# Expert weights by accumulating indirect DMAs into a DRAM table, in place of one-hot products per token

## The reference

```python
def chunk(xc):                                   # 128 tokens; PEER_HEADS = 8, PEER_KEYS = 128, PEER_TOPK = 16
    qh = (xc @ w_query).reshape(PEER_CHUNK, PEER_HEADS, PEER_QDIM)
    s1, s2 = ...                                 # scores against the two halves of the sub-keys
    v1, i1 = lax.top_k(s1, PEER_TOPK)
    v2, i2 = lax.top_k(s2, PEER_TOPK)
    cand = (v1[..., :, None] + v2[..., None, :]).reshape(PEER_CHUNK, PEER_HEADS, 256)
    vs, ci = lax.top_k(cand, PEER_TOPK)
    e1 = jnp.take_along_axis(i1, ci // PEER_TOPK, axis=-1)
    e2 = jnp.take_along_axis(i2, ci % PEER_TOPK, axis=-1)
    idx = e1 * PEER_KEYS + e2                    # one of 16384 experts
    g = jax.nn.softmax(vs, axis=-1)
    z = jnp.einsum('td,thkd->thk', xc, u_experts[idx])
    a = gelu(z) * g
    return jnp.einsum('thk,thkd->td', a, v_experts[idx])
```

## Time and profile before

| | before |
|---|---|
| median of 3 runs, us | 1976.41 (1974.06 to 1978.56) |
| span of the profiled execution, us | 1975.5 |
| mean granted clock of TensorE, share of full | 0.974 |
| PE busy, us | 1858.1 (94%) |
| DVE busy, us | 1457.3 (74%) |
| ACT busy, us | 860.9 (44%) |
| Pool busy, us | 30.0 (2%) |

### The profile page before, as it was taken

One profiled execution on the slowest core, in us unless ns is written; L12 is line 12 of the kernel. 1 busy time (PEld: TensorE's weight loads), 2 busy tenths in 40 slices (PEclk: granted clock), 3 DMA queues, 4 the chain that ended last, 5 costly groups with the idle time before them and its releaser, 6 DMA issues.

```text
span 1975.5 us, 36620 instructions
## 1 busy us (share of the span) xinstructions
PE 1858.1 (94%) x12406; PEld 1700.7 (86%) x12406; DVE 1457.3 (74%) x2826; ACT 860.9 (44%) x1255; POOL 30.0 (2%) x56
## 2 busy tenths in 40 slices
PE   5999899979998999779887999999999999999997
PEld 5999799969997999668776999999999888888885
DVE  4876556658756666665776699998888899996665
ACT  4344344434443444434544455543333333334443
POOL 0000000000000011000000000000000000000000
PEclk9999899989998999979998999999999999999999
DMA  5655465544444777553465455554444444445554
GB/s 189 206 169 181 144 211 185 186 132 163 158 154 146 254 245 214 172 169 123 155 211 193 138 172 180 174 179 137 138 138 138 135 142 148 139 149 172 194 194 142
DMA packets 91534, 334.14 MB, mean 169 GB/s; under 512 B 10697, under 2 KB 10857, under 8 KB 91010
## 3 DMA queue, kind: packets, MB, share of 16 engines
q1 hardware_dynamic: 86976, 314.23, 48.5%
q0 software_dynamic: 3504, 14.69, 2.3%
q10 hardware_dynamic: 978, 4.20, 0.6%
HBM read 330.95 MB, written 6.05 MB: 171 GB/s over the span
## 4 chain that ended last, share of the span: by engine, by line
PE 42%; DVE 12%; issue 2%; ACT 2%; DMA 0%; DVEq 0%; ACTq 0%; SPq 0%
PE bank L183 12%; PE bank L185 12%; PE bank L184 12%; DVE Z L82 5%; PE bank L1274 5%; DVE w_lo L164 4%; ACT w_hi L162 1%; DVE xn L82 1%; PE bank L402 1%; DVE st L82 0%; PE bank L347 0%; DVE rows_a L1259 0%; PE bank L237 0%; DMA raw<-stream 0%; PE bank L1114 0%
## 5 line engine op out<-in xcount | busy, mean ns | idle before, releaser
L164 DVE TENSOR_TENSOR w_lo<-raw,w_hi 128x1024 fp32r<-128x1024 f32 x594 | 718.8, 1222 | 227.3 <-ACT w_hi L162 218.4
L162 ACT ACTIVATE w_hi<-raw 128x1024 fp32r<-128x1024 f32 x594 | 624.7, 1053 | 286.2 <-PE bank L185 253.8
L183 PE MATMUL bank<-u_hi,w_hi 128*128 128x256 f32 x2416 | 700.7, 290 | 10.9 <-DVE cw L82 3.2
L184 PE MATMUL bank<-u_lo,w_hi 128*128 128x256 f32 x2416 | 687.5, 285 | 0.0
L185 PE MATMUL bank<-u_hi,w_lo 128*128 128x256 f32 x2416 | 687.1, 284 | 0.0
L183 PEld LDWEIGHTS bank<-u_hi,w_hi 128*128 128x128 f32 x2416 | 467.1, 193 | 22.8 <-issue 14.3
L184 PEld LDWEIGHTS bank<-u_lo,w_hi 128*128 128x128 f32 x2416 | 467.3, 193 | 4.8 <-issue 2.4
L185 PEld LDWEIGHTS bank<-u_hi,w_lo 128*128 128x128 f32 x2416 | 467.0, 193 | 0.0
L183 PE MATMUL bank<-w_hi,a_hi 128*128 128x512 f32 x768 | 306.6, 399 | 1.9 <-DVE a_lo L1321 1.9
L184 PE MATMUL bank<-w_lo,a_hi 128*128 128x512 f32 x768 | 300.2, 391 | 0.0
L185 PE MATMUL bank<-w_hi,a_lo 128*128 128x512 f32 x768 | 299.8, 390 | 0.0
(11 more groups left out here) (207 smaller groups left out, 1562.9 us busy)
## 6 DMA issues: line engine op xcount, KB each, us to landing
raw<-stream SPq DMA_DIRECT2D x594, 512.0 KB, 3.3
ada<-b_ada POOLq DMA_DIRECT2D x6, 512.0 KB, 5.3
t_rows<-t_by_distance POOLq DMA_DIRECT2D x8, 256.0 KB, 3.2
gains_b<-gains POOLq DMA_DIRECT2D x1, 2048.0 KB, 7.8
rpb_rows<-rpb_pad POOLq DMA_DIRECT2D x8, 224.0 KB, 3.8
gains<-gains POOLq DMA_DIRECT2D x3, 512.0 KB, 5.7
bias_a<-t_rows POOLq DMA_DIRECT2D x1, 1536.0 KB, 9.3
bias_b<-rpb_rows POOLq DMA_DIRECT2D x16, 96.0 KB, 4.8
```

The source lines that it names most:

```text
L162: nc.scalar.activation(w_hi[:, s, :], raw[:, s, :], ACT.Copy).then_inc(s_hi, 1)
L164: nc.vector.tensor_tensor(w_lo[:, s, :], raw[:, s, :], w_hi[:, s, :].bitcast(F32), ALU.subtract).then_inc(s_split, 1)
L183: M.matmul(o, lh, rh, start=start, stop=False, skip_group_check=True)
L184: M.matmul(o, lh, rl, start=False, stop=False, skip_group_check=True)
```

## The change

The one-hot matrices, the maps, `apply`, `weigh` and the transposes are removed. A table of 128 x 128 x 256 floats (16.8 MB) in DRAM, `mix_dram`, is filled with zeros by eight DMAs of the Pool queue, from piece 88 of the first layer on, one every four pieces. A head of the selection now spans 12 up pieces, one step of `select` per piece; at its end the place of each pick in the table (second index x 128 x 256 + first index x 256 + token) and its softmax share are formed. Pool then issues, for each head, 32 indirect DMAs (16 picks x 2 halves of the tokens), each of 128 elements of 4 bytes, one per partition, that add into the table; before the next head it waits until all of the last have landed. After all up pieces but three ACT waits for the last landing and loads the first four tiles of weights; in the down loop it loads each tile four ahead, and DVE multiplies it into `Z` (`gated`) two ahead. Banks 4 to 7 take the up tiles in turn (before: 4 and 5).

```diff
-SEL_PIECES = 8
-FIRST = PH * SEL_PIECES + RING
+SEL_PIECES = 12
+ZERO_COLS, ZERO_PARTS = 512, 8
+        mix_dram = nc.dram_tensor("expert_weights", [PK * P * T, 1], F32, kind="Internal").ap()
...
+        nc.vector.memset(zeros[:, :], 0.0).then_inc(s_zeros, 1)
...
+        G.wait_ge(s_zeros, 1)
+        mix_parts = mix_dram.rearrange("(c p a n) o -> c p a (n o)", c=ZERO_PARTS, p=P, n=ZERO_COLS)
+        for j in range(ZERO_PARTS):
+            after_piece(88 + 4 * j)
+            G.dma_start(mix_parts[j], zeros[:, :].unsqueeze(1).to_broadcast(
+                [P, PK * P * T // (ZERO_PARTS * P * ZERO_COLS), ZERO_COLS])).then_inc(s_zero, 16)
...
         G.wait_ge(s_t5r, 16 * 8)
+        G.wait_ge(s_zero, 16 * ZERO_PARTS)
         G.dma_start(gains_b[:, :, :], gains2.partition_broadcast(P)).then_inc(s_gain2, 16)
...
-            CH.go((m,), V.tensor_copy, best[:, :, bass.ds(h * PT, PT)],
-                  pick[:, 0, :].rearrange("p (t n) -> p t n", t=NT))
+            values = pick[:, 0, :].rearrange("p (t n) -> p t n", t=NT)
+            V.tensor_tensor(diff.rearrange("p (t n) -> p t n", t=NT), values,
+                            values[:, :, 0:1].to_broadcast([P, NT, PT]), ALU.subtract).then_inc(s_diff, 1)
...
+            S.wait_ge(s_diff, h + 1)
+            S.activation(power, diff, ACT.Exp).then_inc(s_exp, 1)
             for side in range(2):
-                CH.go((ms[2 * side + 1],), V.tensor_reduce, rowcol[:, side, :, bass.ds(h * PT, PT)],
-                      e5[side], AX.X, ALU.add)
-                yield
+                m = CH.go((ms[2 * side + 1],), V.tensor_reduce, rowcol[:, side, :], e5[side], AX.X, ALU.add)
+            yield
+            m = CH.go((m,), V.scalar_tensor_tensor, rowcol[:, 0, :], rowcol[:, 0, :], float(T), token,
+                      ALU.mult, ALU.add)
+            CH.wait(m)
+            V.scalar_tensor_tensor(place[:, bass.ds(h, 1), :].rearrange("p a n -> p (a n)"), rowcol[:, 1, :],
+                                   float(P * T), rowcol[:, 0, :], ALU.mult, ALU.add).then_inc(s_picked, 1)
+            V.wait_ge(s_exp, h + 1)
+            p2d = power.rearrange("p (t n) -> p t n", t=NT)
+            m = CH.go((), V.tensor_reduce, smx[:, 0, :], p2d, AX.X, ALU.add)
+            m = CH.go((m,), V.reciprocal, smx[:, 1, :], smx[:, 0, :])
+            CH.wait(m)
+            V.tensor_tensor(share[:, bass.ds(h, 1), :].rearrange("p a (t n) -> p (a t) n", t=NT), p2d,
+                            smx[:, 1, :].unsqueeze(2).to_broadcast([P, NT, PT]), ALU.mult).then_inc(s_picked, 1)
+            yield
...
-                    expert_up(j % 2, h * SEL_PIECES + j)
+                    expert_up(j % RING, h * SEL_PIECES + j)
                     yield
-            weave(ups(), select(h), 2)
+            weave(ups(), select(h))
...
+        G.wait_ge(s_zero, 16 * ZERO_PARTS)
+        for h in range(PH):
+            G.wait_ge(s_picked, 2 * (h + 1))
+            if h:
+                G.wait_ge(s_spread, 16 * NT * PT * h)
+            for n in range(NT * PT):
+                G.indirect_dma_start(
+                    mix_dram, bass.IndirectOffsetOnAxis(ap=place[:, h, n:n + 1], axis=0),
+                    share[:, h, n:n + 1], None, compute_op=ALU.add).then_inc(s_spread, 16)
...
+        def fetch(q, tile):
+            S.dma_start(mix[:, q, :], mix_tiles[bass.ds(tile, 1), :, :].rearrange(
+                "a p t -> (a p) t")).then_inc(s_mix[q], 16)
+        def gated(q, tile, quad):
+            zj = Z[:, bass.ds(tile * T, T)]
+            V.wait_ge(s_mix[q], 16 * quad + 16)
+            V.tensor_tensor(zj, zj, mix[:, q, :], ALU.mult).then_inc(s_m, 1)
         def weighted(q, tile, read):
             zj = Z[:, bass.ds(tile * T, T)]
+            S.wait_ge(s_m, tile + 1)
...
-        def expert_down(q, tile, first=False, last=False, more=True):
-            if more:
-                weighted(1 - q, tile + 1, dyn(RING) + at["piece"])
+        def expert_down(q, quad, first=False, last=False, left=RING):
+            tile = quad * RING + q
+            if left > 2:
+                gated((q + 2) % RING, tile + 2, quad + (q + 2) // RING)
+            if left > 1:
+                weighted((q + 1) % 2, tile + 1, dyn(RING) + at["piece"])
+            if left > RING:
+                S.wait_ge(s_m, tile + 1)
+                fetch(q, tile + RING)
...
+        expert_up(0, PK - RING)
+        S.wait_ge(s_spread, 16 * PH * NT * PT)
+        for j in range(RING):
+            fetch(j, j)
+        expert_up(1, PK - RING + 1)
+        expert_up(2, PK - RING + 2)
+        V.wait_ge(s_z, 2 * RING + 2)
+        gated(0, 0, 0)
         weighted(0, 0, None)
+        expert_up(3, PK - RING + 3)
+        gated(1, 1, 0)
```

More of the change, by code:

```diff
@@ L51 @@
 N_PIECES = LAYERS * N_LAYER + N_ADA + N_MIXER2 + N_QUERY + 2 * PK
-SEL_PIECES = 8
-FIRST = PH * SEL_PIECES + RING
-assert N_LAYER % RING == 0 and N_ADA % RING == 0
+SEL_PIECES = 12
+ZERO_COLS, ZERO_PARTS = 512, 8
+assert N_LAYER % RING == 0 and N_ADA % RING == 0 and SEL_PIECES % RING == 0
 class Line:
@@ L136, in build @@
         s_chain = sem("s_chain")
-        s_ha = sem("s_ha")
-        s_g = sem("s_g")
+        s_zero, s_zeros = sem("s_zero"), sem("s_zeros")
+        s_diff, s_exp, s_picked = sem("s_diff"), sem("s_exp"), sem("s_picked")
+        s_spread = sem("s_spread")
+        s_mix = [sem(f"s_mix{i}") for i in range(RING)]
         s_m = sem("s_m")
@@ L448, in build @@
         relu = qT[:, 0:2, :]
+        zeros = sb(ph1a, "zeros", [P, ZERO_COLS])
         for tt in range(NT):
@@ L1071, in build @@
         Z = sb(ctx, "Z", [P, PK * T])
[L1072 to L1075, removed]
+        place = sb(ctx, "place", [P, PH, NT * PT], U32)
+        share = sb(ctx, "share", [P, PH, NT * PT])
+        mix = sb(ctx, "mix", [P, RING, T])
         qhT = Z[:, 0:N_QUERY * T].rearrange("p (f t) -> p f t", t=T)
@@ L1119, in build @@
             free[b] = (m,)
-        take(0), take(1), take(2), take(3), take(4), take(5)
+        for b in range(8):
+            take(b)
         VE.wait(m)
         CH = Line(nc.vector, s_chain)
-        S.sem_inc(s_z, 2)
+        S.sem_inc(s_z, RING)
         def expert_up(q, tile):
@@ L1211, in build @@
         at["quads"], at["piece"] = quads0, piece0 + PH * SEL_PIECES
-        n0 = PH * SEL_PIECES
[L1215 to L1294, removed]
+        G.wait_ge(s_zero, 16 * ZERO_PARTS)
[7 more added lines that the diff above has]
+                    share[:, h, n:n + 1], None, compute_op=ALU.add).then_inc(s_spread, 16)
@@ L1295, in build @@
+        S.wait_ge(s_picked, 2 * PH)
+        n0 = PH * SEL_PIECES
         quads, piece = at["quads"], at["piece"]
-        with nc.Fori(0, (PK - FIRST) // RING - 2, engines=compute) as i:
+        with nc.Fori(0, (PK - n0) // RING - 1, engines=compute) as i:
             at["quads"], at["piece"] = quads + i, piece
             for j in range(RING):
-                expert_up(j % 2, i * RING + (FIRST + RING + j))
-                apply((j - 1) % 2, i * RING + (2 * RING + j - 1), 0, left)
-                maps(j % 2, i * RING + (2 * RING + j), 0, left)
@@ L1302, in build @@
-        at["quads"], at["piece"] = quads, piece + PK - FIRST - 2 * RING
-        for j in range(RING):
-            expert_up(j % 2, PK - RING + j)
-            apply((j - 1) % 2, total - RING + j - 1, 0, left)
-            maps(j % 2, total - RING + j, 0, left, j < RING - 1)
-        apply(1, total - 1, 0, left)
-        assert (PK - FIRST) + RING == total
-        V.wait_ge(s_z, PK + 2)
-        S.wait_ge(s_m, total)
+                expert_up(j, i * RING + (n0 + j))
+        at["quads"], at["piece"] = quads, piece + PK - n0 - RING
@@ L1336, in build @@
         acc = [[bank[0][:, :], bank[1][:, :]], [bank[2][:, :], bank[3][:, :]]]
+        expert_up(0, PK - RING)
[6 more added lines that the diff above has]
+        gated(0, 0, 0)
         weighted(0, 0, None)
[L1338 removed]
+        expert_up(3, PK - RING + 3)
+        gated(1, 1, 0)
         for j in range(RING):
[L1340 to L1343 removed]
+            expert_down(j, 0, first=j == 0, left=RING + 1)
+        V.wait_ge(s_z, PK + RING)
         quads, piece = at["quads"], at["piece"]
[L1345 removed]
+        with nc.Fori(0, PK // RING - 2, engines=compute) as i:
             at["quads"], at["piece"] = quads + i, piece
             for j in range(RING):
[L1348 to L1363 removed]
+                expert_down(j, i + 1, left=RING + 1)
+        at["quads"], at["piece"] = quads, piece + PK - 2 * RING
         S.wait_ge(s_used, N_PIECES - PK // 2)
@@ L1373, in build @@
         for j in range(RING):
-            n = PK - RING + j
-            m = expert_down(j % 2, n, last=j == RING - 1, more=j < RING - 1)
+            m = expert_down(j, PK // RING - 1, last=j == RING - 1, left=RING - j)
         assert at["piece"] == N_PIECES, (at["piece"], N_PIECES)
@@ L1455, in kept_table @@
     row = np.arange(P, dtype=np.float32)
-    return np.concatenate([np.eye(P, dtype=np.float32), np.tile(row, (P, 1)),
```

(3 more changed lines are left out.)

34 lines of the change are left out of this document (7 added, 27 removed).

## The result

The changed kernel takes 2091.0 us in the median (2089.0 to 2092.6); before, on the same chip, 1977.3 us: a ratio of 1.058, interval 1.056 to 1.059. The forecast was 1856, the range ended at 2015.

The account below looks back on a forecast made before the run. PE, 94% busy, was taken as the bound; without the products, softmax stage and breaks, and with the scatter hidden, break-even stood 121.4 us away and the time at 1856 us (1848 to 1868). The recorded range was 1848 to 2015.

Parts of the forecast that it names:

- part (1): Map products removed: PE gets back 55.7 + 59.5 us, the softmax stage and breaks go too; 716.8 us remain on PE.
- (2): Softmax and place sums moved into the head loop: PE paces at 34.6 us a head, DVE 29.6; 2.4 us excess.
- (3): Down tiles gain a DVE product and an ACT load issue: DVE 2.07 of 2.72 us; first fetch costs 2 us.
- Rival E: Down tiles stay at 3.3 us instead of 2.72, 74 us back, time 1929; chance 0.06.
- (4): Eight zero writes of 2.1 MB by the Pool queue, lasting till some 420 us: cost nothing (0 to 6 us).
- (5): Scatter of 256 indirect DMAs on Pool: at 1.1 us each it ends at 1452, before 1483.4, so PE loses nothing.
- X: Distance of two indirect DMAs on Pool: taken as about 1.1 us; PE loses nothing up to 1.23.
- C: Rival: scatter issue on Pool becomes the bound, slower from 1.70 us a DMA; 2011 us at 1.84, 2078 at 2.1; chance 0.20.
- the forecast's formula: Scatter ends at 1155 + 256 X + 7 L if Pool paces; PE loses 256 (X - 1.23) beyond X = 1.23.
- L: Pool's wait between heads until all of the last head's DMAs landed: at least 2.1 us, taken as 2.1.
- The rule of the Trainium skill: Every Pool issue waits for one DVE low half, 1.22 us on top of 0.62: 1.84 us a DMA, time 2011.
- D: Rival: the DMA engines choke on the adds; break-even 125 ns an add, time 2159 at 176 ns; chance 0.08.

Follow-up runs that it names:

- half_dmas: The changed kernel with only the first 16 of each head's 32 indirect DMAs, picks of tokens 128 to 255 not added: 1851.7 us, ratio 0.937.
- plain_write: The changed kernel with all 256 indirect DMAs writing each share in place of adding it: 1923.2 us.
- dve_beside: The changed kernel with 60 two-input adds, 60 sums and 80 copies given to DVE while only Pool works: 2100.9 us.

## Why the prediction was wrong

**What bounded before, and part (1).** Right. The products are gone, PE's work fell by the named 115 us and some. half_dmas is 124.2 us faster than before on its chip (1975.9 - 1851.7) where the sum said 121.4.

**(2) The heads.** Right. In the changed kernel up tiles stand 2.88 us apart:

```profile
1173.55 0.39 ACT L1143 ACTIVATE Z<-bank 128x256 f32 x1 [1.55 <-PE bank L189]
1176.43 0.39 ACT L1143 ACTIVATE Z<-bank 128x256 f32 x1 [1.55 <-PE bank L189]
...
1187.95 0.39 ACT L1143 ACTIVATE Z<-bank 128x256 f32 x1 [1.55 <-PE bank L189]
1188.36 1.28 ACT L1209 ACT_TABLE_LOAD   x1
1189.65 0.23 ACT L1209 ACTIVATE Z<-Z 128x32 f32<-128x32 f32 x1
1190.85 1.28 ACT L1143 ACT_TABLE_LOAD   x1
```

A head takes 34.55 us = 12 x 2.88 in place of the 34.9 with the taken excess; DVE is 87% busy in the stretch from 1200 us, where 29.6 of 34.6 had been reckoned (86%). The last three rows are an Exp behind a Gelu and the two table loads of 1.28 us around it; nothing on PE moves for them. The 2.4 us taken as excess of the heads didn't come.

**(3) The down tiles.** Right: 2.72 us apart, DVE at 71% (the sum said 76%), and ACT's issue of a load takes 0.34 us, as read from SP's row:

```profile
1809.80 0.42 ACT L1283 ACTIVATE a_hi<-Z 128x256 fp32r x1 [1.06 <-PE bank L189]
1809.96 0.34 ACTq L1268 DMA_DIRECT2D mix<-expert_weights  x1
1812.52 0.42 ACT L1283 ACTIVATE a_hi<-Z 128x256 fp32r x1 [1.06 <-PE bank L189]
```

Rival E didn't occur.

**(4) The zeros.** Right in cost. The DMA digits go to 9 in the slices from 313 to 418 us, and the line from 300 us shows 288 GB/s. What Pool reached at 289.8 and 639.5 us before it reaches at 292.0 and 642.0 after: the shift of 2.2 us was there before the first zero (314.8), and the zeros add 0.3. From 300 to 440 us PE is busy for 127.05 us, before for 127.28.

**(5) The scatter: the step that failed.** X was taken as 1.1 us, "nearer to the plain rows since nothing inside a head waits for a landing". That nothing inside a head waits for a landing is true: the idle before a DMA there is 0.30 us but for the six stops. But the reason says only what is not in the price. X measured 1.85 us bare and 2.10 on average. Its parts are 0.96 us for the issue of an indirect write, 0.59 for the add, 0.30 between two DMAs, where the row of a plain one has only its own 0.49, 0.21 on average for the waits behind DVE's instructions (0.43 in head 0, 2.28 - 1.85), and 0.05 for the stops. The forecast named none of the last four. Even without the add the bare distance is 1.26 us, and plain_write still lost 67.5 us of PE: the guess of 1.1 was near the bare issue of a plain scatter, 0.96, and not near the distance of two.

The bound above, "2.1 us, if every DMA waited for its own landing", came close to the measured mean for a reason that doesn't exist. It was a number by accident; the mechanism that holds is that of C (the Pool queue paces, the point of 1.70 us from which it is slower than before). Put X = 2.10, the mean after the fact, into the forecast's formula: the scatter ends at 1155 + 256 x 2.10 + 14.7 = 1707.3, the loss is 223.9 us and the time 2079. The 12 us to 2091 are small sizes: head 0 picked at 1159.5 and not 1155 (4.5, of which 2.2 are a shift that begins before the zeros and that half_dmas has only in part: its first expert matmul is at 1119.9, not 1121.3), L of 2.9 us on average and not 2.1 (5.5 over seven heads), and from the last landing to the first down matmul 6.8 us (1718.9 to 1725.8) and not 4.5.

**The rule of the Trainium skill.** As the prediction used it, every issue waits for one whole low half on top of a plain DMA's 0.62 us: X = 1.84 and 2011 us. That GpSimd waits for a DVE instruction with two SBUF inputs came true, by dve_beside. But only 80 of the 256 DMAs meet a low half, and they wait for what is left of it, so the waits are worth 0.21 us a DMA and not 1.22. That 1.84 looks like the bare 1.85 is chance: the base price was two and a half times the 0.62, and the base price, not the contention, carried the time over 2011.

**D** didn't occur: where Pool works without the stream, the DMA engines are 21% busy; with it, 60 to 71%, and up tiles keep their 2.88 us.

**The chances.** C had 0.20 and was priced for X between 1.70 and 2.1; the range was cut at 2011, inside of C, because the price at one low half looked like its most. With X unknown between 0.49 and 2.1 and no row of its kind, three fifths of that width lay above 1.1, and everything over 1.23 loses. The margin of 0.13 us between 1.1 and 1.23, on a term that counts 256 times, should have taken the forecast's 0.48 down.

## What to carry to other kernels

Where a change puts hundreds of small DMAs on a queue, their number times the issue price of one is the first thing to set against the work that hides them; an indirect DMA with add took Pool 1.85 us here with 128 indices and still 1.71 with 64, so count instructions first, not bytes. An unknown unit price that enters 256 times deserves a wide range on both sides of the point where cover ends. And where one way is free only up to a number and the other has a constant price, use the first up to that number: that gave the only kernel here that does the whole work and beats the one before.

## What the runs showed of the hardware

- Issue price on Pool of one indirect DMA with one 4-byte element per partition, beside idle engines: 0.96 us writing and 1.55 us adding with 128 indices, 1.41 adding with 64, each followed by 0.30 us before the next. The first one after all others have landed takes no less.
- Beside DVE instructions with two SBUF inputs (0.69 us each) 1.87 us, beside copies of 128x512 floats 1.80, beside reduces 1.55. A DMA that begins inside a two-input instruction is longer by what is left of it less 0.13 us (74 of 80 in the changed kernel, within 0.06 us).
- In return the two-input instructions keep their time; the copies go from 0.423 to 0.487 us on average.
- From a head's last issue to the next head's first, through the landing, 2.1 us beside nothing and 3.0 to 3.9 beside the stream in the changed kernel; in half_dmas, beside the stream throughout, 2.1 to 3.2.
- While PE stood idle its granted clock was 0.50, the lower of its two levels (1.2 GHz). The first matmul after the hole took 0.77 us, where one of the same shape in the earlier trace rows takes 0.39:

```profile
1725.76 0.77 PE L187 MATMUL bank<-w_hi,a_hi 128*128 128x512 f32 x1 [235.55 <-DVE a_lo L1285]
```

The table by stretch, from the first matmul on:

```profile
1725.00:1735.00 10.00, 9.24 (x32) 7.51 (x33) 6.73 (x11) 5.67 (x9) 0.00 (x0) 0.75 0.73 227
1735.00:1745.00 10.00, 10.00 (x46) 8.29 (x45) 7.33 (x11) 4.99 (x8) 0.00 (x0) 1.00 0.73 255
```

In the second ten microseconds the granted clock is back at 1.00, its upper level (2.4 GHz).
